# Splitting the final norm of a hybrid decoder step into three token groups

## The reference, cut to what matters

```python
def _rmsnorm(x, g):
    xf = x.astype(jnp.float32)
    y = xf * lax.rsqrt(jnp.mean(xf * xf, axis=-1, keepdims=True) + EPS)
    return (y * g.astype(jnp.float32)).astype(x.dtype)

for l in range(DEPTH):
    h = _rmsnorm(x, w['norm_mix_g'][l])
    ...
    x = x + jnp.einsum('blm,md->bld', mix, w['w_out'][l])
    h = _rmsnorm(x, w['norm_ffn_g'][l])
    ...
    x = x + jnp.einsum('blf,fd->bld', jax.nn.gelu(gate) * up, w['ffn_w_down'][l])
y = _rmsnorm(x, w['norm_final_g'])
```

## Time and profile before

| what | us |
|---|---|
| median of three runs | 2728.16 |
| the three runs | 2735.53, 2727.76, 2728.16 |
| span of the profiled execution, first to last instruction | 2729.1 |
| TensorE busy in the span | 2685.6 (98%) |
| VectorE busy | 1985.2 (73%) |
| GpSimd busy | 1260.7 (46%) |
| ScalarE busy | 865.7 (32%) |
| TensorE starts its first projection product | 9.72 |
| TensorE ends the last product of layer 1 | 2707.77 |
| VectorE starts its first output tile | 2715.26 |
| VectorE ends its last output tile | 2725.41 |

### The profile page before, as it was taken

The page is one execution under the profiler, slowest core; times in us unless marked ns, Lnnn a source line. Parts: engine busy times, 40 slices in busy tenths (PEclk is TensorE's granted clock), DMA queues, the critical chain, the costliest instruction groups (busy, mean ns, idle before and its releaser), DMA issues.

```text
span 2729.1 us, 51065 instructions
## 1 busy us (share of the span) xinstructions
PE 2685.6 (98%) x18801; PEld 2636.6 (97%) x18801; DVE 1985.2 (73%) x2490; ACT 865.7 (32%) x1380; POOL 1260.7 (46%) x732
## 2 busy tenths in 40 slices
PE   9999999999999999999999999999999999999997
PEld 9999999989999999999999999999999999999997
DVE  7658898478876666667946598875788666677778
ACT  4333231124322232223423342312343322233333
POOL 2333333212665666666533333232226666666663
PEclk9999999999999999999999999999999999999999
DMA  4324333321211111111223244244111111111112
GB/s 167 129 78 152 125 128 128 113 70 32 63 51 49 46 46 46 48 60 47 67 91 107 95 150 143 89 142 134 42 39 55 46 46 51 57 46 46 46 62 92
DMA packets 74103, 220.12 MB, mean 81 GB/s; under 512 B 18480, under 2 KB 19632, under 8 KB 72896
## 3 DMA queue, kind: packets, MB, share of 16 engines
q1 hardware_dynamic: 69584, 202.80, 22.8%
q10 hardware_dynamic: 4368, 15.33, 1.9%
HBM read 176.87 MB, written 41.73 MB: 80 GB/s over the span
## 4 chain that ended last, share of the span: by engine, by line
PE 57%; issue 18%; POOL 13%; DVE 7%; DMA 2%; ACT 1%; PEld 1%; POOLq 0%; DVEq 0%; SPq 0%; ACTq 0%
PE ps L909 17%; PE ps L911 16%; PE ps L910 16%; POOL sb_w_lo L812 9%; DMA sb_w_raw<-w 2%; DVE sb_pt L1947 1%; POOL sb_w_raw L855 1%; POOL sb_wsum L844 1%; DVE sb_x L1937 1%; POOL sb_w_raw L851 1%; PE ps L1043 1%; POOL sb_rawx L847 1%; PE ps L1157 1%; PE ps L1078 1%; PE ps L1079 1%
## 5 line engine op out<-in xcount | busy, mean ns | idle before, releaser
L812 POOL TENSOR_TENSOR sb_w_lo<-sb_w_raw,sb_w_hi 128x512 fp32r<-128x512 f32 (+1 forms) x348 | 640.4, 1845 | 426.1 <-ACT sb_w_hi L1735 418.5
L909 PE MATMUL ps<-sb_p_hi,sb_w_hi 128*128 128x258 f32 (+1 forms) x2528 | 729.7, 289 | 9.3 <-POOL sb_w_lo L812 8.6
L911 PE MATMUL ps<-sb_p_hi,sb_w_lo 128*128 128x258 f32 (+1 forms) x2528 | 726.5, 287 | 0.0
L910 PE MATMUL ps<-sb_p_lo,sb_w_hi 128*128 128x258 f32 (+1 forms) x2528 | 726.1, 287 | 0.0
L809 POOL TENSOR_TENSOR sb_w_hi<-sb_w_raw,sb_ones 128x1024 fp32r<-128x1024 f32 (+1 forms) x92 | 178.7, 1942 | 859.7 <-PEq L906 749.5
L909 PE MATMUL ps<-sb_h_hi,sb_w_hi 128*128 128x344 f32 x1632 | 535.8, 328 | 3.9 <-DVE sb_h_lo L1899 1.8
L910 PE MATMUL ps<-sb_h_lo,sb_w_hi 128*128 128x344 f32 x1632 | 524.0, 321 | 0.0
L911 PE MATMUL ps<-sb_h_hi,sb_w_lo 128*128 128x344 f32 x1632 | 522.4, 320 | 0.0
L909 PEld LDWEIGHTS ps<-sb_p_hi,sb_w_hi 128*128 128x128 f32 x2528 | 477.9, 189 | 11.8 <-POOL sb_w_lo L812 10.4
L910 PEld LDWEIGHTS ps<-sb_p_lo,sb_w_hi 128*128 128x128 f32 x2528 | 479.4, 190 | 0.0
L911 PEld LDWEIGHTS ps<-sb_p_hi,sb_w_lo 128*128 128x128 f32 x2528 | 478.2, 189 | 0.0
(11 more groups left out here) (336 smaller groups left out, 3695.6 us busy)
## 6 DMA issues: line engine op xcount, KB each, us to landing
sb_w_raw<-w SPq DMA_DIRECT2D x178, 512.0 KB, 3.8
proj<-sb_ev SPq DMA_DIRECT2D x56, 516.0 KB, 3.0
sb_rawx<-w SPq DMA_DIRECT2D x44, 512.0 KB, 3.5
sb_pt<-proj SPq DMA_DIRECT2D x20, 516.0 KB, 4.9
sb_raw<-proj SPq DMA_DIRECT2D x16, 516.0 KB, 4.5
sb_raw<-proj ACTq DMA_DIRECT2D x16, 516.0 KB, 4.3
sb_ch<-cumT SPq DMA_DIRECT2D x32, 256.0 KB, 3.9
sb_raw<-ssd_state SPq DMA_DIRECT2D x4, 1024.0 KB, 6.3
```

Of the source, the lines that this page charges most:

```text
L812: return nc.gpsimd.tensor_tensor(o, a, h.bitcast(F32), ALU.subtract)
L909: mm(o, wh, ah, start=first, stop=False)
L910: mm(o, wh, al, start=False, stop=False)
L911: return mm(o, wl, ah, start=False, stop=last)
```

## The change

The code is changed in four places.

1. The last down piece (tile 7) of each layer is computed one token group after the other (384, 384 and 264 tokens) and not one contraction step after the other. VectorE adds each group to `x`, ScalarE squares it (`last_square`), VectorE adds the square to `rstd` (`last_add`), group by group.
2. The normed halves of tiles 6 and 7 are made at the loop's head and no longer at the layer's end. The same holds for layer 0: in the start section tiles 6 and 7 are left out, all squares and adds come first, and then the head of the loop makes their halves. TensorE's order at the head is changed: step 5 of tile 1 comes ahead of step 5 of tile 0, and the count that frees the first weight buffer (`w_used0`) comes after step 6 of tile 1 and not after step 5.
3. The final norm goes by group: three small sums for each group, a square root that adds the epsilon by its bias, a reciprocal, three transposes to a bank for VectorE and three more to another bank, from which ScalarE copies the spread value to `tab` for GpSimd. The four matmuls on ones go. A one-element square root in each layer's end has ScalarE load that table.
4. The output tiles are written by group, 24 pieces. VectorE makes 19 of them. GpSimd makes five: tiles 5 and 6 in groups 0 and 1, tile 5 in group 2, from tiles that ScalarE has scaled by the gain (`fpt`). SyncE issues 19 DMAs and ScalarE five.

Two instructions lose an increment that nobody waits for, and a tile `eps` of two columns is added ahead of the large tiles.

```diff
+    eps = sb("eps", [P, 2])
+    LAST_CHUNKS = [(0, 128, 256), (384, 512, 640), (768, 896, T - CHUNK)]
+    COPY_BANK = [3, 4, 3]
+    POOL_TILES = [(5, 6), (5, 6), (5,)]
 @sync
-        for m in range(KD):
-            for n, s in enumerate(parts(m)):
-                sp.wait_ge(*sg.after("y_ready", (m, n)))
+        for g in range(NG):
+            for m in y_tiles(g):
+                sp.wait_ge(*sg.after("y_ready", (m, g)))
                 step()
-                sp.dma_start(io["y"][m][:, s], out_tile(m)[:, s])
+                sp.dma_start(io["y"][m][:, tg(g)], out_tile(m)[:, tg(g)])
 @gpsimd
+        for g in range(NG):
+            pool.wait_ge(*sg.after("rstd_half", ("last", g)))
+            for m in POOL_TILES[g]:
+                pool.wait_ge(*sg.after("rstd_half", ("y", m)))
+                nc.gpsimd.tensor_tensor(out_tile(m)[:, tg(g)], out_tile(m)[:, tg(g)], tab[:, tg(g)], ALU.mult)
 @tensor
             for k in range(5):
                 tile_k(0, 1, k, False)
+            pe.wait_ge(sg.sem("h_split"), layer * KD + 6)
+            tile_k(0, 1, 5, False)
             for k in range(5, KD):
                 pe.wait_ge(sg.sem("h_split"), layer * KD + (k + 1))
                 ins = tile_k(4, 0, k, k == KD - 1)
-            for k in range(5, KD):
+            for k in range(6, KD):
                 ins = tile_k(0, 1, k, k == KD - 1)
-                if k == 5:
+                if k == 6:
                     ins.then_inc(sg.sem("w_used0"), 1)
...
+        last_sums(0)
+        last_sums(1)
+        last_spread(0)
+        last_sums(2)
+        spread_again(0)
+        last_spread(1)
+        spread_again(1)
+        last_spread(2)
+        spread_again(2)
 @scalar
             act.wait_ge(*sg.after(f"x_loaded{m}"))
-            part(m, 0, "start")
-        for m in range(KD):
+            if m < KD - 2:
+                part(m, 0, "start")
+        for m in range(KD - 1):
             square(m, "start")
+        for g in range(NG):
+            last_square(g, "start")
         with act.Fori(0, DEPTH) as layer, sg.loop("layer", DEPTH, layer):
+            for m in (KD - 2, KD - 1):
+                part(m, layer * 2, "top")
...
+            square(KD - 2, "next")
+            af(eps[:, 1:2], ones[:, 0:1], ACT.Sqrt)
+            for g in range(NG):
+                act.wait_ge(*(sg.after("sq_used", ("x", g)) if g < NG - 1 else d_freed(layer, LOOPED, 5 + KD - 1)))
+                last_square(g, "next")
+        for m in (5, 6):
+            af(out_tile(m), x[:, m, :], ACT.Identity, scale=gain(m, 2 * DEPTH))
+        last_root(0)
+        last_root(1)
+        copy_rstd(0)
+        last_root(2)
+        copy_rstd(1)
+        copy_rstd(2)
+        for g in range(NG):
+            store_pool(g)
 @vector
+        for g in range(NG):
+            last_add(g, "start")
         with dve.Fori(0, DEPTH) as layer, sg.loop("layer", DEPTH, layer):
-            v.tensor_tensor(rstd[:], rstd[:], ev[:, 1, :], ALU.add).then_inc(*sg.on("sums_done"))
+            for m in (KD - 2, KD - 1):
+                part(m, layer * 2, "top")
...
+            add_square(KD - 2, "next")
+            for g in range(NG):
+                if g < NG - 1:
+                    dve.wait_ge(*sg.after("last_part", g))
+                else:
+                    piece_done(LOOPED, 15 + 11)
+                xg = x[:, KD - 1, tg(g)]
+                ins = v.tensor_tensor(xg, ps[:, g, 0:DT[g][1]], xg, ALU.add)
+                last_add(g, "next")
+        last_rstd(0)
+        last_rstd(1)
+        dve.wait_ge(*sg.after("spread", 0))
+        scale_out(0, y_tiles(0)[:2])
+        last_rstd(2)
+        scale_out(0, y_tiles(0)[2:])
+        for g in (1, 2):
+            dve.wait_ge(*sg.after("spread", g))
+            scale_out(g, y_tiles(g))
```

More of the change, by code:

```diff
@@ L517, in spill @@
                 if i == 24:
[L518 removed]
+                    sp.wait_ge(*sg.after("tile_scaled", 0))
                 elif i == 25:
[L520 removed]
+                    sp.wait_ge(*sg.after("tile_scaled", 1))
                 else:
@@ L1194, in _ @@
             pe.wait_ge(*sg.after("ones_ready"))
-            pe.wait_ge(*sg.after("sums_done"))
+            pe.wait_ge(*sums_ready(layer))
             token_sums("mix", "w_used1")
@@ L1358, in _ @@
                 down_piece(LOOPED, p, 14 + p // 2, 2 * (p % 2), [Yf(p >= 4)])
-            for p in range(KD, 12):
+            for p in range(KD, 11):
                 entry_ready(LOOPED, 10 + p)
                 down_piece(LOOPED, p, 10 + p, 0, [Yf(False), Yf(True)])
[L1362 to L1378, removed]
+            entry_ready(LOOPED, 21)
@@ new lines, in _, with last_sums, spread_to @@
+            pe.wait_ge(*d_freed(layer, LOOPED, 10))
+            last_piece()
+        def last_sums(g):
+            pe.wait_ge(*sg.after("sums_part", ("next", g)))
+            for n, c0 in enumerate(LAST_CHUNKS[g]):
+                ins = mm(ps[:, 5 + g, n:n + 1], rstd[:, c0:c0 + CHUNK], ones[:, 0:1], start=True, stop=True)
+            ins.then_inc(*sg.on("tok_sum", ("last", g)))
+        def spread_to(bank, g):
+            for n, c0 in enumerate(LAST_CHUNKS[g]):
+                at = c0 - DT[g][0]
+                ins = nc.tensor.transpose(ps[:, bank, at:at + CHUNK],
+                                          rt[:, NG * g + n:NG * g + n + 1].to_broadcast([P, P]), ident)
+            return ins
@@ new lines, in last_spread, with spread_again @@
+        def last_spread(g):
+            pe.wait_ge(*sg.after("tok_rstd", ("last", g)))
+            spread_to(g, g).then_inc(*sg.on("spread", g))
+        def spread_again(g):
+            if g == 2:
+                pe.wait_ge(*sg.after("rstd_half", ("last", 0)))
+            spread_to(COPY_BANK[g], g).then_inc(*sg.on("spread", ("copy", g)))
+        last_sums(0)
[5 more added lines that the diff above has]
+        spread_again(1)
@@ L1397, in part, with last_square @@
             af(h_hi[:, m, :], x[:, m, :], ACT.Identity, scale=gain(m, g)).then_inc(*sg.on("h_hi", (key, m)))
+        def last_square(g, key):
+            if g == 0:
+                act.wait_ge(*sg.after("sq_used", (key, KD - 3)))
+            af(ev[:, 1, tg(g)], x[:, KD - 1, tg(g)], ACT.Square).then_inc(*sg.on("sq_tile", (key, "last", g)))
         def refresh(m, g, key):
             square(m, key)
-            if m == KD - 2:
-                act.wait_ge(sg.sem("f_done"), layer * PIECES + PIECES)
             part(m, g, key)
@@ L2653, in _ @@
             v.nop().then_inc(*sg.on("par_free"))
-            for mo in range(KD):
+            for mo in range(KD - 1):
                 if mo < 4:
                     dve.wait_ge(*d_freed(layer, LOOPED, mo + 1))
-                if mo == KD - 1:
-                    add_square(mo - 1, "next")
                 down(LOOPED, 4 + mo, mo)
-                if mo == KD - 1:
-                    part(mo - 1, layer * 2 + 2, "next")
-                elif mo >= 1:
+                if mo >= 1:
                     refresh(mo - 1, layer * 2 + 2, "next")
-            part(KD - 1, layer * 2 + 2, "next")
@@ new lines, in last_rstd, with scale_out @@
+        def last_rstd(g):
+            dve.wait_ge(*sg.after("tok_root", ("last", g)))
+            v.reciprocal(rt[:, NG * g:NG * g + NG], rt[:, NG * g:NG * g + NG]).then_inc(*sg.on("tok_rstd", ("last", g)))
+        def scale_out(g, ms):
+            for m in ms:
+                gp = gains[:, 2 * DEPTH * KD + m:2 * DEPTH * KD + m + 1]
+                stt(out_tile(m)[:, tg(g)], x[:, m, tg(g)], gp, ps[:, g, 0:DT[g][1]], ALU.mult,
+                    ALU.mult).then_inc(*sg.on("y_ready", (m, g)))
```

104 lines of the change are left out of this document (61 added, 43 removed).

## The result

The changed kernel takes 2740.28 us (median of 7 runs, 2739.05 to 2742.83); the kernel before, on the same chip, 2729.07 (7 runs, 2727.76 to 2735.59). The ratio is 1.0032, 95% interval 1.0023 to 1.0041; it compares all runs of the two kernels and is not the quotient of the medians, which is 1.0041. So the change is slower by 6 to 11 us, about the 0.3% that the prediction took as the least a measurement can tell, and the median is 8 us later than forecast. The two profiled executions, 2740.4 against 2729.1 us, lie at the upper end of that: there are 11.3 us to find in them.

What follows compares the result with a forecast made beforehand. TensorE, busy 98% of the span, was taken to bound the kernel. A start loss of 2.6 us and an end loss of 1.6 made 4.2 on 2728.2, so 2732.4 us, counted as no change; range 2727.4 to 2736.2.

Steps and rivals of the forecast that it cites:

- It waits until 29.35: 2.6 us.: Start: TensorE, ready at 26.7, waits for VectorE's h_lo of tile 6; 2.6 us, bounds 1.0 and 3.5.
- h_hi 6 at 27.75: Start: ScalarE's squares end at 26.6 and its half of tile 6 is done at 27.75, before VectorE's.
- That wait is the term.: Start: the 2.6 us wait is the whole cost there, and no fixed time later takes it up.
- The boundary: nothing.: Boundary of the layers: no cost; tile 6's half is needed at 1378 and made by 1371.3, 6.7 us of cover.
- The end costs 1.6 us: After TensorE's last product: the last landing comes 1.6 us later; bounds minus 0.8 and plus 3.5.
- GpSimd's hold on group 0's add: End: VectorE's add of group 0's square waits for GpSimd's L812, running 2710.24 to 2710.75; without it the end costs 0.4.
- the stall after two pieces: End: VectorE waits 0.9 us for group 2's square root, held on ScalarE behind the copy of group 0.
- The DMA decides: plus 1.6: End: 3.83 MB flow from about 2720.2 at 400 GB/s in 9.6 us, ending at 2729.8 against 2728.2.
- rival 3: Output DMA: short rows lower the rate, slower by over 0.3%; at 200 GB/s the time is 2743; chance 7%.
- Something over the whole length: Whole kernel: buffers moved by a few bytes change the time beyond 8 us in either direction; chance 3%.
- a stage that differs by over a microsecond: Sign of being wrong: any stage between start and end that differs by more than a microsecond.
- rivals 1 and 2: 1: end 0.8 us shorter, start still loses 2.6, 2730.0, 18%. 2: start does not stall, end alone remains, 2729.8, 7%.

Runs made afterwards that it cites:

- the head alone: Kernel before with only the halves of tiles 6 and 7 moved to the loop's head: 2735.4 us, ratio 1.0013 to the kernel before.
- the roots first: Changed kernel with ScalarE's three square roots ahead of its two full-width scalings, TensorE's and VectorE's orders to match: 2740.58 us, ratio 1.0031 to the kernel before.
- the run with the matmuls on ones: Changed kernel with nine unused matmuls on ones ahead of TensorE's wait for tile 6's half, in both layers: 2749.85 us, ratio 1.006 to the kernel before.
- both repairs: Changed kernel with a square root as ScalarE's first start operation and the three final roots ahead of its two scalings: 2740.82 us, ratio 1.0016 to the kernel before.
- the third batch: Third batch of follow-up runs, in which the unchanged kernel before had a median of 2735.2 us.

## Why the prediction was wrong

- **"It waits until 29.35: 2.6 us."** The place, the cause and the adds were right. ScalarE's part was not: "h_hi 6 at 27.75" assumed that the loop is entered with the table loaded, and the load made it 28.7 or so. The wait was 3.26, within the bounds.
- **"That wait is the term."** This is the step that failed. Behind the wait the clock fell, and that cost nearly as much again: 2.8 us in the changed kernel's trace, shown twice, by filling the wait and by shortening it; 1.5 us in the two other traces with a wait of 3.42 (the head alone, and the roots first). The prediction priced the wait by its length and not by what TensorE does after it, though the kernel before shows the pattern itself: its idle of 2.86 before 2045.77 is followed by 3.4 us at the half clock, which is what the 0.67 of this window comes to:

```profile
2045.77 0.43 PE L909 MATMUL ps<-sb_p_hi,sb_w_hi 128*128 128x344 f32 x1 [2.86 <-POOL sb_w_lo L812]
2045.00:2050.00 5.00, 4.23 (x17) 4.24 (x18) 4.93 (x3) 2.88 (x5) 4.92 (x4) 0.67 0.37 105
```

- **The sum with what was measured.** With 6.3 in place of 2.6, and everything else as it was put, the sum would have been 2736.1; with the end's 3.5 as well, 2738.0; with the 1.5 between and the later median of before (2729.07, not 2728.16), 2740.4.
- **"The boundary: nothing."** Right, to 0.35 us. What VectorE waits for at the loop's head (4.87) is ScalarE's half, not its own jump back, as the prediction had it; both halves are done at 1376.3, 5 us ahead of TensorE's need for the first (6.7 put).
- **"The end costs 1.6 us": 3.5 measured.** Its terms: first output 8.9 after the last product, measured 8.73; GpSimd's hold on group 0's add, which was there (1.54 for a 384-column add beside L821); the stall after two pieces 0.9, measured 1.35; VectorE's end 1.7 later, measured 1.8. Then "The DMA decides: plus 1.6" at 400 GB/s failed, though the DMA does decide: the transfers start again 12.9 us after the last product (12.4 put) and take 10.8 us (9.6 put), 355 GB/s on average. In it are the lower rate and, at the end, SyncE's late issues, which the prediction did not price; the runs do not part the two. The mechanism of rival 3 was thus at work with a tenth off the rate (4.23 MB at 366 GB/s are 11.6 us, not 10.6), where it had been given 7% for a much larger drop.
- **Two rules of the Trainium skill.** The rule of the Trainium skill's page "SBUF — State Buffer" (Who interferes with whom) held in the add of 1.54, and GpSimd's five products left VectorE's at 0.54 a piece. The prediction put its second half too widely: the page frees a VectorE instruction with a single SBUF input only outside the two-port modes, and the two that took 1.94 and 2.42 in the run with the matmuls on ones have one such input. The three cycles that the Trainium skill's page "DMA: Bandwidth & Descriptors" (Why small descriptors are slow) gives each packet made 4% more a byte, an estimate; the runs show about 10%.
- **"Something over the whole length."** Between the start and the last product the change has 1.5 us more, made up of 2.9 less and 4.4 more. The prediction named a stage that differs by over a microsecond as a sign of being wrong, and this is one. Executions differ by as much in where the clock falls: at the idle of 2.86 before 696.51 it stayed up in the kernel before, at the same one (2.88, before 701.19) it fell in the change, and at the next (2045.77 and 2051.69) it was the other way round. None of this difference is shown to be of the change.
- **The chances.** The forecast's 65% with rivals 1 and 2 (18 and 7) make 90% for "within 0.3%", not the "91 to 92%" of the text.

The forecast's range ended at 2736.2, above all because the bounds of the start held the wait only: with 6.3 for the start, its upper end would have been 2739.0. The 1.5 us between, beyond the 1 allowed for it, and the later median of before make up the rest.

What stays open: whether any of those 1.5 us belongs to the change, and what decides in an execution whether the clock falls at a recurring idle, and for how long. At the end it is how much of the loss is the lower rate of short rows and how much the late issues.

## What to carry to other kernels

Price a new TensorE wait of two to three microseconds as the wait and possibly 1.5 to 3 us more for the clock behind it, and look in the trace of before for an idle like it to see what followed. Work moved to a loop's head inherits the activation table of both ways into the loop; load the back edge's table first. Cutting an output into small pieces pays only while neither the queue's issue nor the transfer rate is the bound: here whole tiles went at 400 GB/s, and pieces with rows of 1 to 1.5 KB at about 360, with an issue of 0.5 to 1 us each.

## What the runs showed of the hardware

- TensorE's granted clock fell to 1.2 GHz (0.50) behind idles of 3.20 us and more in every trace here, and at an idle of 2.9 in some and not in others. Behind shorter ones it went either way: it stayed at 2.4 GHz behind 1.83, 2.01 and 2.08 and fell behind 1.74 (both repairs, 1367.42), 2.22, 2.23 and 2.25. It also fell where no idle was over 1.5 us (at 602.8 and 1889.6 in the kernel before). So 2 us is no bound that one could plan with. The fall at the start cost 2.8 us in the change, and 1.5 in the three traces where the half clock lasted half as long (the head alone, the roots first, both repairs).
- The scatter of this kernel goes with it. The executions of the kernel before in the third batch, sorted by their mean granted clock, average 2743 (0.992, one run), 2738 (0.993, 8), 2736 (0.994, 7), 2732 (0.995, 5) and 2730 (0.996, 2); 0.001 of 2687 us of TensorE is 2.7 us. In the other kernels with many runs the time goes with the clock in much the same way, so a median of three to seven runs can carry several microseconds of how often the clock fell. That the falls cause all of this is not shown, as the waits behind which the clock falls cost time themselves.
- Moving all large buffers by 8 bytes changed an undisturbed FFN block from 63.07 to 62.90 us, in all seven kernels here that have that tile; the cause was not looked for. The gain is partly lost again: TensorE's idle for GpSimd's halves is 8.5 to 12.7 us in those seven traces and 7.1 to 10.0 in the five without the tile, two ranges that overlap.
